# One table set for logarithm and exponential, loaded at the head of each hybrid layer

## The reference, cut to what matters

```python
def hybrid_layer(h, ...):
    u = rms_norm(h, norm_g)
    dq, dk, dv, dz, fq, fk, fv, fz, f_logit = split(u @ w_in)      # 4 x 128 columns each, f_logit 8
    lam = exp(sum(lam_q1 * lam_k1)) - exp(sum(lam_q2 * lam_k2)) + lambda_init
    # differential heads: two softmaxes, the second times lam is taken off the first
    p = softmax(mask(q1 @ k1.T / 8)) - lam * softmax(mask(q2 @ k2.T / 8))
    o_a = rms_norm(p @ v_a, subln_g) * (1 - lambda_init)
    # forgetting heads: a cumulated log-sigmoid is added to the scores
    cum = cumsum(log_sigmoid(f_logit + b_forget))
    o_b = softmax(mask(q_f @ k_f.T / 8 + cum_q - cum_k)) @ v_f
    return h + concat(o_a * silu(dz), o_b * silu(fz)) @ w_out
```

## Time and profile before

| | |
|---|---|
| median of 3 runs | 2113.77 us (2110.63 to 2114.10) |
| profiled execution, its own time | 2107.99 us |
| profiled execution, span | 2106.2 us |
| TensorE busy | 1939.2 us, 92% |
| VectorE busy | 556.3 us, 26% |
| ScalarE busy | 416.1 us, 20% |
| first hybrid layer, tile products and attention | from 1661.8 us to 1844.4 us |
| second hybrid layer, the same part | from 1893.8 us to 2069.9 us |

### The profile page before, as it was taken

One profiled execution on the slowest core, in us unless ns is written; L12 is line 12 of the kernel. 1 busy time (PEld: TensorE's weight loads), 2 busy tenths in 40 slices (PEclk: granted clock), 3 DMA queues, 4 the chain that ended last, 5 costly groups with the idle time before them and its releaser, 6 DMA issues.

```text
span 2106.2 us, 21632 instructions
## 1 busy us (share of the span) xinstructions
PE 1939.2 (92%) x8583; PEld 1426.7 (68%) x8583; DVE 556.3 (26%) x1339; ACT 416.1 (20%) x989; POOL 56.4 (3%) x68
## 2 busy tenths in 40 slices
PE   6999899787689999999998889989999899999998
PEld 4777678666546777677776677847777667737774
DVE  1000202453311000200005853430000343623344
ACT  1000200132111000200006720340000234312431
POOL 0200000000000000000000303000000000000000
PEclk9999999755589999999999985699999999999999
DMA  5745534200033444445453230023545675366630
GB/s 201 246 151 178 124 120 120 100 1 1 0 98 122 137 162 148 133 138 173 127 168 96 95 106 21 1 80 102 178 132 144 112 115 97 74 105 82 101 101 20
DMA packets 190869, 232.21 MB, mean 110 GB/s; under 512 B 22868, under 2 KB 172696, under 8 KB 190792
## 3 DMA queue, kind: packets, MB, share of 16 engines
q1 hardware_dynamic: 188032, 223.85, 38.9%
q0 software_dynamic: 1840, 5.12, 0.8%
q10 hardware_dynamic: 920, 2.16, 0.3%
HBM read 230.07 MB, written 1.05 MB: 110 GB/s over the span
## 4 chain that ended last, share of the span: by engine, by line
PE 63%; DVE 4%; PEld 2%; issue 2%; ACT 2%; POOL 0%; PEldq 0%; DVEq 0%
PE ps L501 22%; PE ps L274 14%; PE ps L519 10%; PE ps L458 5%; PEld ps L274 2%; PE ps L1548 1%; PE ps L1399 1%; PE ps L542 1%; PE ps L2022 1%; PE ps L2038 1%; PE ps L2026 1%; PE ps L1565 1%; PE ps L357 1%; PE ps L2052 1%; PE ps L2057 1%
## 5 line engine op out<-in xcount | busy, mean ns | idle before, releaser
L501 PE MATMUL ps<-hT,ring 128*128 128x256 f32 x2816 | 624.0, 380 | 0.7 <-issue 0.7
L501 PEld LDWEIGHTS ps<-hT,ring 128*128 128x128 f32 x2816 | 536.8, 191 | 108.3 <-issue 39.3
L274 PE MATMUL ps<-hT,ring 128*128 128x272 f32 (+3 forms) x1408 | 334.6, 392 | 5.5 <-issue 3.0
L274 PEld LDWEIGHTS ps<-hT,ring 128*128 128x128 f32 (+2 forms) x1408 | 256.0, 185 | 67.0 <-issue 11.7
L519 PE MATMUL ps<-ring,arena 128*128 128x512 f32 x640 | 287.7, 592 | 0.0
L573 DVE TENSOR_TENSOR arena<-arena,ps 128x256 f32<-128x256 f32 x88 | 37.1, 421 | 850.5 <-ACT arena L558 850.5
L519 PEld LDWEIGHTS ps<-ring,arena 128*128 128x128 f32 x640 | 121.6, 190 | 118.9 <-issue 114.8
L558 ACT ACTIVATE arena<-ps 128x256 f32<-128x256 f32 x88 | 33.8, 384 | 845.0 <-PE ps L501 845.0
L274 PE MATMUL ps<-arena 128*128 128x64 f32 (+6 forms) x384 | 104.3, 439 | 16.5 <-DVE arena L1261 12.7
L458 PE MATMUL ps<-ring,arena 128*128 128x512 f32 (+1 forms) x256 | 112.6, 596 | 1.5 <-ACT arena L2087 0.8
L274 PEld LDWEIGHTS ps<-arena 128*128 128x128 f32 (+2 forms) x384 | 83.9, 309 | 33.0 <-DVE arena L1261 14.8
(11 more groups left out here) (355 smaller groups left out, 1645.6 us busy)
## 6 DMA issues: line engine op xcount, KB each, us to landing
ring<-in_ffn_w_gate SPq DMA_DIRECT2D x44, 1024.0 KB, 5.3
ring<-in_ffn_w_up SPq DMA_DIRECT2D x44, 1024.0 KB, 5.4
ring<-in_ffn_w_down SPq DMA_DIRECT2D x44, 1024.0 KB, 5.0
ring<-in_w_in SPq DMA_DIRECT2D x32, 1024.0 KB, 10.7
ring<-in_ab_w_in SPq DMA_DIRECT2D x13, 1024.0 KB, 5.4
ring<-in_w_out SPq DMA_DIRECT2D x8, 1024.0 KB, 5.0
ring<-in_ab_w_out SPq DMA_DIRECT2D x6, 1024.0 KB, 5.1
ring<-in_c_w_k SPq DMA_DIRECT2D x4, 1024.0 KB, 5.6
```

The costliest lines, as they stand in the source:

```text
L274: last = nc.tensor.matmul(o, l, r, start=(i == 0), stop=(i == len(pairs) - 1))
L501: m = nc.tensor.matmul(ps[:, 4 + j % 2, 256 * w:256 * (w + 1)], slot8(s0 + 3 * q + w)[:, k, c * P:(c + 1) * P], hT[:, k, META:], start=(k ...
```

## The change

One line at the head of `hybrid_act`. It loads the table set that holds both Ln and Exp. The program builder then finds every function of the layer's loop in the loaded set and places no load inside the loop. The computation is the same, with Exp and Ln taken from that set.

```diff
@@ -2070,6 +2070,7 @@
             units, steps, norms = h_units(layer), h_steps(layer), norm_steps(layer)
             n0, lo = act_u.n, 0 if layer == 0 else META
             act_u.n += len(units)
+            nc.scalar.preload_act_table_set("natural_log_exp_and_others")
             for p in range(len(FT)):
                 kind, i = FT[p]
                 n = act_f()
```

## The result

| | before | after |
|---|---|---|
| median | 2111.31 us (7 runs, 2108.76 to 2114.10) | 2118.01 us (7 runs, 2114.22 to 2119.71) |
| profiled execution, own time | 2107.99 us | 2117.64 us |
| span | 2106.2 us | 2115.8 us |
| TensorE busy | 1939.2 us | 1946.2 us |
| ScalarE busy | 416.1 us | 389.8 us |

The changed kernel is slower by 0.26%: the ratio on record is 1.0026, with a 95% interval of 1.0014 to 1.0038. (It isn't the quotient of the two medians, which is 1.0032.) The forecast was "no change", 2113.6 us. The time lies 0.01 us above the upper end of the range, 2118, and "slower" had a chance of 0.05.

The account below looks back on a forecast made before the run. TensorE, busy 92% of the span, was taken as the bound, with 10.2 us idle in the two hybrid windows. Terms of 0 and 0 left the profiled execution at 2107.99 us; the median was forecast at 2113.6, range 2107 to 2118.

Parts of the forecast that it names:

- 22 loads at no gain: Hybrid layers' loops: removing 22 table loads of 1283 ns wins 0 us, at most TensorE's 10.2 us of idle time.
- margins of 3.65, 3.35 and 2.35 us: First layer's first norm and forget gates: spare time between ScalarE's or VectorE's work ending and TensorE's next use.
- Two new loads at no cost: One load at each hybrid layer's head, hidden in ScalarE's 4.04 us idle time under TensorE's first tile product: 0 us.
- VectorE's wait of 2.73 us: First layer's softmax, behind the fourth load: would shrink to well under 1 us, with nothing gained by TensorE.
- three signs: Forecast wrong if a window shortens over 1 us, an L2073 load exceeds 1.3 us, or an L2111 exponential exceeds 0.41 us.
- What the change removes: Prediction's paragraph on the hybrid layers: 22 loads go, 2 come, 25.7 us less ScalarE time, all else in the same order.
- the sum: Whole kernel: 0 for 22 loads plus 0 for 2 loads leaves the profiled execution at 2107.99 us.
- Rival 2: Layer heads: the new set's load waits for a DMA, up to 18.8 us slower in all; chance 0.03.
- Rival 1: Hybrid loops: loads were on the path, up to 25.7 us faster; chance 0.07 for 4 us and more, 0.01 for all.
- Other harm or luck of the comparison: No place named: any other shift of the time beyond 0.2%; chance 0.02.

Follow-up runs that it names:

- the broadcasts paced: GpSimd's nine 512 KB broadcasts spaced by freed weight slots, small ones behind them: kernel before 2109.40 us, ratio 0.9984; changed kernel 2109.07 us, 0.9982.
- the repeats: Both kernels run again word for word: changed kernel 2117.55 us, ratio 1.0020; kernel before 2112.58 us, ratio 1.0001.
- the joint set everywhere: Changed kernel with the joint set also in the mixer and recurrent mixer, sigmoid's set for Tanh, four sets in all: 2090.64 us, ratio 0.9897 to kernel before.
- The run with eight: Changed kernel plus the Gelu and Mish sets loaded once each behind the last hybrid layer: 2106.87 us, ratio 0.9984 to the kernel before.
- no logarithm: Kernel before with Copy in place of Ln at L2095 and L2118, so 20 loads fewer and no added set: 2114.86 us, ratio 1.0002.

## Why the prediction was wrong

**The steps on the instructions held.**
- 22 loads at no gain: the windows are unchanged, and with the broadcasts paced the two kernels differ by 0.33 us in the median. That fits the margins of 3.65, 3.35 and 2.35 us behind the loads: TensorE gained nothing when the loads went.
- Two new loads at no cost: 1.28 us each, the first over 2 us ahead of the tile copy behind it.
- ScalarE's busy time fell by 26.3 us (25.7 said), VectorE's wait of 2.73 us is gone ("well under 1 us" said), and the exponentials take 0.40 us for 0.41. None of the three signs that the text named as proof against it appeared.

**The step that failed is the last sentence under "What the change removes": "Everything else on all engines stands in the same order, and no DMA or semaphore is moved."** That is true of the instructions, and the sum took it to mean that everything else keeps its time. The sum, 0 for the 22 loads and 0 for the 2, prices the joint set by its two loads alone and lacks a term for the program having a sixth table set. In the two traces it is 2.8 us at 105 us (3.05 us of longer wait, less the 0.3 that the kernel was ahead), 5.65 - 2.77 = 2.9 us of lower clock behind it, 3.2 us of lower clock at 315 us, and 0.8 us in small pieces later: 9.7 us. In medians, where about half of the kernel before's executions have the lower mean clock too, it is 5.0 us (the repeats) and 6.7 us (the first comparison). How a further set slows the burst stays open.

**Rival 2 had the right sign and the wrong mechanism.** It held that the new set could cost time only where its load executes. The load took 1.28 us. The harm of a further set came about 1,570 us earlier, in a burst of GpSimd's queue, and was there as well when the load stood behind all hybrid layers. The trace had the warning: the earlier trace rows show a DMA of 64 KB that took 16.8 us to land. I used it as a price, and never asked what kept the DMA engines so busy there, nor that the weights which TensorE needs next were in the same crowd (0.67 us of wait at 105 us).

**Rival 1 fell**, as argued: no load of the hybrid layers was on the path.

**The chances.** "Other harm or luck of the comparison" got 0.02, and a harm it was. The executions of the kernel before range from 2106.80 to 2117.25 us; the spread that was known, 2107.99 to 2114.10, I read as noise of the level, but it goes with the clock groups. The median of 2113.77 that the forecast starts from lay between them, and the next comparison gave 2111.31. Of the traces in the table, those with a lag of 1.55 us or more at 118 us all fell to the lower clock near 315 us, and those with 1.43 us or less didn't. These are twelve traces, read afterwards. They suggest that an edit which has nothing to do with a place can still tip the clock there.

## What to carry to other kernels

Before you explain a difference, line up the two traces by TensorE's instructions and see where the lag arises; here it was all in place over 1,000 us ahead of the edit. Where a burst of broadcasts saturates the DMA engines beside weights that are just in time, hold the broadcasts back until they are needed: it brought 0.16% to the kernel before, and freed the changed one of its whole loss. Table loads are worth grouping where TensorE waits for ScalarE; that and the clock behind it brought 27 us in the traced execution with the joint set everywhere (2107.99 to 2079.50 us, less the 1.8 us of the burst), though three of that kernel's six executions were near 2098 us; and the hybrid layers, with 2.35 us of margin or more, gave nothing.

## What was unexpected of the hardware

- A further table set in a program changed the rate of unrelated DMAs, and not in the order of the number of sets: 322 to 325 GB/s in the burst with five sets, 305 to 314 with six, 340 with eight, 337 with four. The Trainium skill, "ScalarE activation tables: per-element evaluation and per-set limits", section "Table sets in the compiler and the runtime", names a limit of eight sets per program. The run with eight agrees as far as it goes: its load groups still show 1283 ns each; none had nine.
- The eight broadcasts of 256 bytes to 128 partitions travel as 128 packets of 2048 bytes. In total these took 43.4 us before and 60.8 us after, 339 and 475 ns each; with four sets 23.7 us, 185 ns each; with eight 15.1 us, 118 ns each.
- One wait of TensorE of 3.0 to 4.0 us in an otherwise full stream went with the lower clock in all six traces that have it; it fell 0.1 to 1.2 us before the wait's end. Waits of 0.7 to 1.8 us at the same place didn't, in four traces, though one of these four (no logarithm) lost 6.0 us further on all the same. The clock's price in the six, 1.6 to 3.0 us at once and 3.8 to 6.0 us further on (lag at 700 us less lag at 118 us), is as large as that of the wait.
